# Expert loop of a two-block network: the next rows' transposes and first weight splits moved into the thin blocks, and Silu for sigmoid and product

## The reference, cut to what matters

```python
def expert_block(args):          # xb: up to 128 rows of one expert e
    xb, e = args
    gt = jnp.minimum(xb @ w_gate[e] + b_gate[e], SWIGLU_LIMIT)               # limit 7.0
    up = jnp.clip(xb @ w_up[e] + b_up[e], -SWIGLU_LIMIT, SWIGLU_LIMIT)
    hid = gt * jax.nn.sigmoid(SWIGLU_ALPHA * gt) * (up + 1.0)                # alpha 1.702
    return hid @ w_down[e] + b_down[e]
...
out = jnp.zeros((T + 1, D), x.dtype).at[row_tok].add(y_rows * row_gate[:, None])[:T]
```

## Time and profile before

| | |
|---|---|
| median of three runs | 3174.34 us (3172.1 to 3174.94) |
| the profiled execution | 3175.11 us, of which the span of its instructions 3173.4 us |
| TensorE busy over the span | 93% |
| VectorE, ScalarE, GpSimd busy | 70%, 46%, 17% |
| DMA engines busy in the last third of the span | 8 to 9 tenths in all slices but the last |

### The profile page before, as it was taken

The page is one execution under the profiler, slowest core; times in us unless marked ns, Lnnn a source line. Parts: engine busy times, 40 slices in busy tenths (PEclk is TensorE's granted clock), DMA queues, the critical chain, the costliest instruction groups (busy, mean ns, idle before and its releaser), DMA issues. The chain is left out here.

```text
span 3173.4 us, 46265 instructions
## 1 busy us (share of the span) xinstructions
PE 2956.2 (93%) x16534; PEld 2461.1 (78%) x16534; DVE 2229.9 (70%) x3651; ACT 1444.0 (46%) x1989; POOL 551.0 (17%) x483
## 2 busy tenths in 40 slices
PE   8999899999999999999999887889999998999998
PEld 7997778999998888888888766656666666666666
DVE  6998826993977888888888556555665555565477
ACT  4454624344963333333333353445544445554465
POOL 0000004453003222222222000111111111111111
PEclk9999899999999999999999998899999999999999
DMA  5230113344568999999998214799999999999995
GB/s 149 80 83 31 73 62 136 122 151 159 214 250 332 353 348 347 335 345 347 346 345 312 99 58 165 271 383 383 391 389 376 366 387 385 384 382 379 357 396 207
DMA packets 192684, 846.93 MB, mean 267 GB/s; under 512 B 20048, under 2 KB 101584, under 8 KB 148993
## 3 DMA queue, kind: packets, MB, share of 16 engines
q1 hardware_dynamic: 165600, 694.50, 56.7%
q0 software_dynamic: 26976, 151.03, 13.4%
HBM read 798.79 MB, written 56.62 MB: 270 GB/s over the span
## 5 line engine op out<-in xcount | busy, mean ns | idle before, releaser
L3606 DVE TENSOR_TENSOR moe_w_lo<-all_raw,moe_w_hi 128x2048 fp32r<-128x2048 f32 x178 | 402.3, 2286 | 101.7 <-ACT moe_w_hi L3493 101.1
L3493 ACT ACTIVATE moe_w_hi<-all_raw 128x2048 fp32r<-128x2048 f32 x178 | 335.6, 1911 | 41.6 <-DMA all_raw<-in_w_moe 19.0
L1984 ACT ACTIVATE experts_wu_hi<-all_wu 128x1024 fp32r<-128x1024 f32 x128 | 135.7, 1060 | 250.9 <-PE experts_Y L1936 242.6
L1330 POOL TENSOR_TENSOR score_w_lo<-all_hT,score_w_hi 128x1024 fp32r<-128x1024 f32 x59 | 146.0, 2477 | 584.0 <-DVE all_x_lo L1479 459.9
L1904 POOL DMA_INDIRECT experts_pair<-in_peer_pairs,experts_slot x128 | 145.5, 1136 | 552.4 <-DVE all_h L2088 539.3
L3383 PE MATMUL moe_GU<-moe_w_hi,moe_x_hi 128*128 128x512 f32 x576 | 235.7, 409 | 0.0
L3384 PE MATMUL moe_GU<-moe_w_lo,moe_x_hi 128*128 128x512 f32 x576 | 235.0, 408 | 0.0
L3385 PE MATMUL moe_GU<-moe_w_hi,moe_x_lo 128*128 128x512 f32 x576 | 233.5, 405 | 0.0
L2062 DVE TENSOR_TENSOR experts_wu_lo<-all_wu,experts_wu_hi 128x1024 fp32r<-128x1024 f32 x128 | 156.8, 1225 | 62.1 <-ACT experts_wu_hi L1984 60.0
L1925 PE MATMUL experts_H<-all_x_hi,experts_wd_hi 128*128 128x384 f32 x504 | 169.8, 337 | 2.1 <-DVE experts_wd_lo L2058 2.1
L1927 PE MATMUL experts_H<-all_x_hi,experts_wd_lo 128*128 128x384 f32 x504 | 169.8, 337 | 0.0
(11 more groups left out here) (628 smaller groups left out, 7689.9 us busy)
## 6 DMA issues: line engine op xcount, KB each, us to landing
all_raw<-in_w_moe SPq DMA_DIRECT2D x149, 2048.0 KB, 13.0
all_hT<-in_w_moe SPq DMA_DIRECT2D x49, 2048.0 KB, 11.8
all_wu<-in_peer_pairs SPq DMA_DIRECT2D x64, 1024.0 KB, 7.4
all_hT<-in_peer_wdT SPq DMA_DIRECT2D x122, 512.0 KB, 9.7
peer_gates<-gates_out SPq DMA_DIRECT2D x6, 4096.0 KB, 12.2
experts_gt<-peer_gates SPq DMA_DIRECT2D x32, 768.0 KB, 9.3
all_hT<-in_w_in SPq DMA_DIRECT2D x40, 512.0 KB, 3.8
all_hid<-peer_early SPq DMA_DIRECT2D x60, 192.0 KB, 4.9
```

Of the source, the lines that this page charges most:

```text
L3493: act.activation(w_hi[p % RING][:], piece_of(r, p), ACT.Copy).then_inc(w_high, 1)
L3606: dve.tensor_tensor(w_lo[p % RING][:], piece_of(r, p), w_hi[p % RING][:].bitcast(F32), ALU.subtract).then_inc(w_low, 1)
```

## The change

Five edits, in the wide and thin blocks of the expert stage:

1. TensorE turns the next wide block's rows behind chunk T1 of the thin block, and no longer behind T4.
2. ScalarE and VectorE split these rows (`x_part`) earlier in the thin block, and ScalarE makes the high parts of the next wide block's first two pieces ahead of the copy of the thin result.
3. The second transposes of the hidden rows come later: in the wide block by three matmuls, in the thin block inside T4 (before its last two matmuls).
4. `Silu` of 1.702 g, which is 1.702 g times its sigmoid, takes the place of the sigmoid and of VectorE's product; the factor 1/1.702 goes into the splits or the copy of the hidden rows.
5. The chain counter of VectorE counts one step per half, not two.

```diff
 # TensorE, wide block
                             for f in range(2):
-                                if p == 9 and f == 1:
-                                    turn_hidden(wide, 1)
                                 h = HT * (q - 4) + 2 * second + f
                                 for b in range(2):
+                                    if p == 9 and f == 1 and b == 1:
+                                        turn_hidden(wide, 1)
...
 # TensorE, thin block
+                                if q == 4 and f == 2:
+                                    turn_thin_hidden(i, 1)
                         mm.then_inc(thin_done, 1)
+                        if q == 1:
+                            turn(0, i + 1)
                         if q == 2:
                             turn_thin_hidden(i, 0)
-                        if q == 4:
-                            turn_thin_hidden(i, 1)
-                            turn(0, i + 1)
...
 # ScalarE
-                    act.activation(sg, ga[:], ACT.Sigmoid, scale=SWIGLU).then_inc(sig, 1)
+                    act.activation(sg, ga[:], ACT.Silu, scale=SWIGLU).then_inc(sig, 1)
...
-                    act.activation(h_split(hid_hi, half), h_turned(half), ACT.Copy).then_inc(h_high, 1)
+                    act.activation(h_split(hid_hi, half), h_turned(half), ACT.Copy, scale=1 / SWIGLU).then_inc(h_high, 1)
...
-                    for half in range(2):
-                        thin_sigmoid(i, half)
-                        thin_hidden(i, half)
+                    thin_sigmoid(i, 0)
                     x_part(i * 2 + 2)
+                    thin_hidden(i, 0)
+                    thin_sigmoid(i, 1)
+                    thin_hidden(i, 1)
+                    high(2 * CHUNKS, i, i + 1, 0)
+                    high(2 * CHUNKS, i, i + 1, 1)
                     act.wait_ge(thin_done, i * CHUNKS + 2 * CHUNKS)
                     act.wait_ge(filed, i * 2 + 2)
                     act.activation(y[:, 1, 0:CHUNK], Y[:, 0, :], ACT.Copy, scale=slot[:, 1, 2:3].bitcast(F32)).then_inc(y_ok, 1)
-                    for p in range(RING):
-                        high(2 * CHUNKS, i, i + 1, p)
+                    high(2 * CHUNKS, i, i + 1, 2)
+                    high(2 * CHUNKS, i, i + 1, 3)
...
 # VectorE, wide unit (the thin unit alike)
-                    dve.tensor_tensor(ga[:], ga[:], sg, ALU.mult).then_inc(h_chain, 1)
-                    dve.wait_ge(h_chain, wide * 4 + (2 * half + 2))
-                    dve.scalar_tensor_tensor(out=hid, in0=up[:], scalar=1.0, in1=ga[:],
+                    dve.wait_ge(h_chain, wide * 2 + (half + 1))
+                    dve.scalar_tensor_tensor(out=hid, in0=up[:], scalar=1.0, in1=sg,
...
-                    dve.tensor_tensor(h_split(hid_lo, half), h_turned(half), h_split(hid_hi, half).bitcast(F32),
-                                      ALU.subtract).then_inc(h_low, 1)
+                    dve.scalar_tensor_tensor(out=h_split(hid_lo, half), in0=h_turned(half), scalar=1 / SWIGLU,
+                                             in1=h_split(hid_hi, half).bitcast(F32), op0=ALU.mult, op1=ALU.subtract).then_inc(h_low, 1)
...
-                    for half in range(2):
-                        thin_gate(i, half)
-                        thin_unit(i, half)
-                    dve.wait_ge(thin_in, i * 2 + 2)
+                    thin_gate(i, 0)
+                    thin_unit(i, 0)
+                    x_part(i * 2 + 2)
+                    thin_gate(i, 1)
+                    thin_unit(i, 1)
                     pick_bias(i * 2 + 2)
-                    x_part(i * 2 + 2)
```

More of the change, by code:

```diff
@@ L3505, in sigmoid @@
                     act.wait_ge(g_ok, wide * 2 + (half + 1))
-                    act.activation(sg, ga[:], ACT.Sigmoid, scale=SWIGLU).then_inc(sig, 1)
+                    act.activation(sg, ga[:], ACT.Silu, scale=SWIGLU).then_inc(sig, 1)
                 def hidden(wide, half):
                     act.wait_ge(turned, wide * 2 + (half + 1))
-                    act.activation(h_split(hid_hi, half), h_turned(half), ACT.Copy).then_inc(h_high, 1)
+                    act.activation(h_split(hid_hi, half), h_turned(half), ACT.Copy, scale=1 / SWIGLU).then_inc(h_high, 1)
                 def thin_sigmoid(i, half):
                     act.wait_ge(thin_g, i * 2 + (half + 1))
-                    act.activation(sg[:, 0:CHUNK // 2], ga[:, 0:CHUNK // 2], ACT.Sigmoid, scale=SWIGLU).then_inc(thin_sig, 1)
+                    act.activation(sg[:, 0:CHUNK // 2], ga[:, 0:CHUNK // 2], ACT.Silu, scale=SWIGLU).then_inc(thin_sig, 1)
                 def thin_hidden(i, half):
@@ L3518, in thin_hidden @@
                     act.activation(thin_hid(half).rearrange("p (s f) t -> p f s t", s=2),
-                                   thin_turn(half).rearrange("p (f s t) -> p f s t", f=2, s=2), ACT.Copy).then_inc(thin_in, 1)
+                                   thin_turn(half).rearrange("p (f s t) -> p f s t", f=2, s=2), ACT.Copy,
+                                   scale=1 / SWIGLU).then_inc(thin_in, 1)
                 def wide_pieces(first, i, wide):
@@ L3655, in thin_unit @@
                     dve.wait_ge(thin_sig, i * 2 + (half + 1))
-                    dve.tensor_tensor(ga[:, thin], ga[:, thin], sg[:, thin], ALU.mult).then_inc(thin_chain, 1)
-                    dve.wait_ge(thin_chain, i * 4 + (2 * half + 2))
-                    dve.scalar_tensor_tensor(out=hid[:, thin], in0=up[:, thin], scalar=1.0, in1=ga[:, thin],
+                    dve.wait_ge(thin_chain, i * 2 + (half + 1))
+                    dve.scalar_tensor_tensor(out=hid[:, thin], in0=up[:, thin], scalar=1.0, in1=sg[:, thin],
                                              op0=ALU.add, op1=ALU.mult).then_inc(thin_h, 1)
```

## The result

The changed kernel takes 3268.35 us (median of four runs, 3263.09 to 3272.17) against 3173.85 us (median of four; the table above has three of them): ratio 1.030, 95% interval 1.028 to 1.032, slower by 94 us. The forecast was 3222, at most 3254: the direction was right, the size about half of what came. The profiled execution took 3266.21 us.

A forecast was written before the change was run, and what follows sets the result against it. TensorE and the DMA engines were both taken as nearly full in the expert loop. TensorE's +3.1 us and the weights' +3.5 gave +3.4 a round, 51 us over fifteen, less 2 and 0.8: 3222 us, range 3191 to 3254.

The forecast's parts named there:

- The turn moved ahead of T2: Thin block: TensorE asks for the next wide block's rows at +7.8, they land at +17.0; wait 9.2 us a round.
- The clock: Thin block, behind the gather wait: TensorE at half clock loses 2.1 us, counted equal to the loss behind today's pause.
- The gap at the wide block's start: First wide-block matmul: its first piece is split before the thin block ends, so the 5.0 us pause shrinks to 0.2, -4.8 us.
- Silu and the later turn: Turning of the hidden rows: VectorE's chain behind W'3 shortens by 2.1 us, TensorE's waits go, -1.3 us a round.
- Sum by TensorE: Expert loop: TensorE's terms 9.2 - 4.8 - 1.3 + 0 make each round +3.1 us.
- Check by the weights: Expert loop: weight landings put the next thin block at +72.4 against 68.9, so +3.5 us a round.
- the landing of W'0: Weight queue in the thin block: W'0 lands an estimated 6.2 us after issue, bounds 4.9 and 13.0 us.
- the 2.9 us of interference: Weight queue from W'0 to W'3: scatter and gather of the thin rows take some 2.9 us of that stretch.
- the closing term: End of the round: from W'3's landing to the next thin block, 26.7 us today minus 2.1, so 24.6 us.
- the cold and dry case: Weight queue dry twice a round, wait 10.4 us, 8.4 us at half clock: 3.3 us more a round, 3272 us; chance 0.16.
- the case of the other side: Rival: the gather comes early; under 2.9 us there is no wait, 3141 us. Chance of anything faster 0.06.

The follow-up runs named there:

- light weights: Loads of W'0 to W'5 bring only half of each chunk: kernel before 3156.44 us (ratio 0.994), changed kernel 3219.62 us (ratio 1.014).
- Where four loads were asked for at once: Changed kernel with early gather, W'0 to W'3 all waiting for the end of T5 instead of T2 to T5 one by one: 3266.77 us, ratio 1.029.

## Why the prediction was right in its first half and wrong in its size

**The turn moved ahead of T2**: right. Forecast turn at +17.0, wait 9.2 us; here +16.6, and 133.0 us in fifteen, 8.9 us. The gather's issue at +4.9 did not move.

**The clock**: right. 2.1 us a round, for which the run with 36 matmuls without use shows 31 us over fifteen.

**The gap at the wide block's start**: right in its mechanism and instants (T2 done forecast +24.0, here +23.8; thin end forecast +35.8, here +35.6; wide start +36.0, here +36.0). The pause of 5 us became 0.5.

**Silu and the later turn**: Silu alone took the waits at the hidden rows from 19.1 to 3.4 us. In the changed kernel the 1.3 us a round did not come: the waits of 13.9, 11.8 and 9.7 us, 2.4 us a round, stand where the sum had 0.2, since the pieces come late. The runs with light weights don't test this term, because there these waits are gone without Silu too (rounds of 67.7 us in the kernel before).

**Sum by TensorE**, +3.1 us a round: it comes out with light weights, at 71.9 us (68.9 + 3.0). With full weights it is short by those new waits.

**Check by the weights**: this is the step that failed. It gave +3.5 us and so seemed to agree; measured is +6.2 us. By its own terms, in the round at 2490.75 and by medians of the fourteen whole rounds:

| | forecast | this round | median |
|---|---|---|---|
| W'0 asked for | +24.0 | +24.0 | +24.2 |
| W'0 there | +30.2 | +31.6 (7.7 us, not 6.2) | +31.9 |
| W'1 there | +35.1 | +37.7 (6.1 us later, not 4.9) | +38.1 |
| W'2 there | not given; +40.0 at 4.9 us, more with interference | +42.6 | +42.9 |
| W'3 there | +47.8 | +48.1 | +48.5 |
| from W'3 to the next thin block | 24.6 | 26.7 | 26.6 |
| next thin block | +72.4 | +74.8 | +75.1 |

The landings of this round come from these answers, the loads issued at 2514.73, 2519.13, 2523.1, 2526.5 and 2529.12 (W'0 to W'4):

```profile
DMA to landing us min/median/max: 7.7/7.7/7.7
...
DMA to landing us min/median/max: 9.3/9.3/9.3
...
DMA to landing us min/median/max: 10.2/10.2/10.2
...
DMA to landing us min/median/max: 12.3/12.3/12.3
...
DMA to landing us min/median/max: 16.5/16.5/16.5
```

Two terms are mis-sized. The first is the landing of W'0, which the prediction called an estimate of 6.2 us with a lower bound of 4.9: it took 7.5 to 7.8 us in all fourteen rounds, and W'1, asked for 4.4 us after it, came 6.2 us behind it and not 4.9. Together with the issue, 0.2 us later, that makes W'1 3.0 us late, and W'2 2.9. Where four loads were asked for at once, only the first came slowly; why W'0 itself takes 7.7 us stays open.

The second is the closing term. By the prediction's own sum the first fault hardly shows, because W'3 was only 0.7 us late: the 2.9 us of interference that it put before W'3 fell there in part only. The scatter and the gather of the thin rows are issued at +37.4 and +41.1 (medians; +26.2 and +30.3 in the kernel before), and W'4 comes 6.2 us behind W'3 where it was 4.9. That these two belong together is likely, and no run tests it. But the prediction then added 26.7 - 2.1 = 24.6 us behind W'3, as if the shortened chain there ended last, and 26.6 us it was. What ends last is VectorE. From the first low part of W'2 on its stretch is 22.9 us, of which it idles 0.2 us (24.1 us in the kernel before, which has the two products as well). In all six versions that have the other edits and full weights, with rounds from 65.7 to 75.1 us, the next thin block starts 32.1 to 32.8 us after W'2 is there (medians). Along that path W'2 at +40.0 gives 72.1 us, and W'2 at +42.9 the 75.0 us that came. That the prediction's own closing gave nearly the first number is chance.

The prediction put the cold and dry case at 0.16, with the words "the sum above has both dry spells already". It had the dry spells and not the refilling. That case's 3272 us are near the 3268 that came, but by luck: its own terms, a wait of 10.4 us and 8.4 us at half clock, did not come (8.9 and 4.4 us).

Another fault is one of weighing. Two sums of which the longer decides both stood at 72. A term that comes out too small in either makes the round longer, while one that comes out too large makes it shorter only if the other sum shrinks too. The forecast should have lain above both, and the range further up. Two small slips besides: the terms add up to 3223 and not 3222, and halfway of the cold case is 3247 and not 3250.

**The rivals.** The gather did not come early: 10.3 us was the least of thirty. With the gather moved, the case of the other side did arrive, 3130 us, where I had 3141 for it. By the rule in "DMA: Bandwidth & Descriptors", section "Anatomy of one DMA — SWDGE (gpsimd) path", of the Trainium skill, 2 us plus bytes over 436 GB/s, this round's gather would have taken some 3.2 us, an estimate for 128 rows. The trace has 11.6 us for it, and the trace decides.

## What to carry to other kernels

Before an instruction that waits is moved ahead, look at when what it waits for is *issued*, and by whom: here a gather behind a scatter behind the result of the block before. Where several resources are near full, work out the round by each of them, and take more than the longest. Follow the arrival behind which nothing idles any more, and not one chosen beforehand: VectorE is busy 70% of the span before, and yet it is what closes each round. A transfer queue that is kept from asking for its next buffer pays the idle time and then the refill: here 7.7 and 6.2 us for two chunks that take 4.9 each in a full queue. With light weights, two thirds of the loss were TensorE's wait all the same. And the cure lay on an idle engine: moving the gather took 138 us off the changed kernel. By itself that reordering is worth 12 to 16 us, the other edits are worth 25, and the early turn, which made the loss, is worth nothing even with its rows in time.
